# A two-block transformer kernel: inh, the gate weights and the ring 96 bytes further on in SBUF, everything behind them 128 bytes

## The chip, the core and the metric

The kernel runs on one core of one Trainium2 chip. The metric is the device time of one execution in microseconds; lower is better. The kernel before takes 1469.38 us, the median of three runs.

## What is computed

The reference takes one sequence of 256 tokens with 1024 features in float32 through two blocks and normalises at the end. The first block is an RWKV-7 recurrence beside a sparse attention with compressed, selected and window branches, and a gated feed-forward layer. The second has two layers, one with a gated linear attention beside a softmax attention with forget gates ("even"), one with an attention over a selected latent ("odd"), with two half-weighted feed-forward layers in each. Cut to what carries the time:

```python
h = h + y @ w_out[i]
h = h + swiglu(rms_norm(h, norm2_g[i]), ffn_w_gate[i], ffn_w_up[i], ffn_w_down[i])
...
x = x + 0.5 * swiglu_2(rmsnorm(x, g[0]), ffn_w_in[layer, 0], ffn_w_out[layer, 0])
h = rmsnorm(x, g[1])
x = x + even_mixer(h, ...)   # or odd_mixer
x = x + 0.5 * swiglu_2(rmsnorm(x, g[2]), ffn_w_in[layer, 1], ffn_w_out[layer, 1])
```

There are five feed-forward layers, each with a hidden width of 2816, and three input projections (w_in, even_in, odd_in) with an output projection each.

## The kernel before

All weights come as one stream of slots of 128 x 3072 floats (12,288 bytes in a partition) through a ring of four slots in SBUF, loaded by the SyncE queue; a slot is loaded again when its user frees it. The five engines run programs written out by hand, tied by semaphores.

A float32 product is made of three passes over split operands. ScalarE copies a block of weights, rounded to the type fp32r, out of the ring (the high half). VectorE subtracts that from the block, which leaves the low half. The activations are split in the same way: uT_h lies in the tensor uT, uT_l in yT. The passes are high weights by high activations, low by high, high by low. Where the halves lie depends on the stage:

- w_in: high in `in_h` (the tensor inh), low written back into the ring, `ring_r` (hi_block L1289, lo_block L1946). In its column items the weights are stationary and uT, 256 columns, is moving; in its token items it is the other way round. 22 column items of 24 matmuls each and two token items of 24.
- even_in and odd_in: high in `even_h` and `odd_h`, which lie in the scratch tensor wk, low in `ring_r`.
- output projections: high in `out_h` (in wk), low in `ring_r`; both moving, 512 columns, with uT stationary.
- feed-forward layers (five times 22 chunks): both halves in `w_gu` and `w_dn`, which lie in wk. A chunk is 48 matmuls with w_gu stationary and uT moving (256 columns), then 12 with the hidden values `h_r` (in ffb) stationary and w_dn moving (512 columns). ScalarE copies the high half (L1303, L1309), VectorE subtracts (L1953, L1959).

Almost all matmuls are issued by the helper at L440, so groups are told apart by their tiles: in "ps<-uT_h,w_gu" ps is the PSUM bank that is written, the others are the two operands.

inh, gate_r and the ring are used as scratch too: inh holds attention scores and probabilities outside w_in. The SBUF tensors are laid down one after the other with the helper `sb`; views made with `over` (in_h, ring_r, w_gu, h_r and so on) move with the tensor under them. The allocator rounds each start up to a multiple of 32 bytes.

Of the kernel before, what the change touches and what calls it, by code (L numbers as in the profile page):

```python
# [15 lines left out]
P = 128  # L16
# [76 lines left out]
def build(nc, x_in, wstream, gains, consts_in, masks_in, scratch, out):  # L93
    ctx = ExitStack()
    with ctx:
        at = {}

        def sb(name, shape, dt=F32):
            at[name] = nc.sbuf_base
            return ctx.enter_context(nc.sbuf_tensor(name, shape, dt))  # L100
# [19 lines left out]
        xn = sb("xn", [P, TT, D])  # L120
        uT = sb("uT", [P, KC, T])
        yT = sb("yT", [P, KC, T])
        inh = sb("inh", [P, KC * 3 * P])
        gb = inh[:, 0:2 * D].rearrange("p (a b) -> p a b", b=D)
        sb("gate_r", [P, 2 * KC * 24])
        ring = sb("ring", [P, RING, SLOT])
        ffb = sb("ffb", [P, 4, T])
        cst = sb("cst", [P, NCONST])
        msk = sb("msk", [P, MASKS], U8)
# [2549 lines left out]
```

## Time and profile before

| | |
|---|---|
| median of three runs | 1469.38 us (1469.09 to 1470.21) |
| the profiled execution | 1469.0 us |
| its span | 1467.2 us |
| TensorE matmul busy | 1427.4 us (97%) |
| weight loads busy | 1313.1 us (89%) |
| VectorE busy | 958.4 us (65%) |
| ScalarE busy | 698.3 us (48%) |
| read from HBM | 235.89 MB, 162 GB/s over the span |

In the profile PE is TensorE's matmuls, PEld its weight loads, DVE VectorE, ACT ScalarE, SP the queue that issues the transfers. L440 is line 440 of the kernel. Times in the timeline count from the span's start. Matmuls are pipelined: the printed duration of one is modelled, and the distance from one start to the next is what it costs in a dense stretch.

### The profile page before, as it was taken

To read this page: it belongs to the slowest core of one execution; us is meant where nothing else is said; L and a number is where in the kernel's file an instruction comes from. 1 tells how busy PE (TensorE), PEld (TensorE's weight loads), DVE (VectorE), ACT (ScalarE), POOL (GpSimd) and SP (SyncE) were. 2 spreads that over 40 slices of the span, in tenths; PEclk is the share of its full clock that TensorE was granted. 3 is DMA by queue.
4 is the path that set the end of the run, shared out by engine and by line. 5 is a ranking of instruction groups with operands and counts; after the bars stand their busy time and mean duration, and the time that the engine had idled before them with its cause. 6 is when DMAs were issued, how large, how long until landed. Compare 5 with 4: busy or idle time off the path is not lost. (4 is left out here: it accounts for less than half of the span.)

```text
span 1467.2 us, 26041 instructions
## 1 busy us (share of the span) xinstructions
PE 1427.4 (97%) x10266; PEld 1313.1 (89%) x10266; DVE 958.4 (65%) x1559; ACT 698.3 (48%) x1119; POOL 86.9 (6%) x140
## 2 busy tenths in 40 slices
PE   8998999999999999999999999999999999999998
PEld 7886998899998999989989999999999878899997
DVE  4766657766667766666467666676665667576665
ACT  6763444543345434457564434353433656544342
POOL 2040001000002000010000000010000114000000
PEclk9999999999999999999999999999999999999999
DMA  8343001654553545424336545445545423455440
GB/s 347 142 157 130 1 1 44 244 212 175 186 201 130 216 176 201 180 96 163 130 121 246 193 176 201 182 166 184 205 176 189 161 86 140 149 216 195 172 171 29
DMA packets 26575, 238.06 MB, mean 162 GB/s; under 512 B 2544, under 2 KB 6784, under 8 KB 7808
## 3 DMA queue, kind: packets, MB, share of 16 engines
q1 hardware_dynamic: 23824, 233.39, 43.1%
q10 hardware_dynamic: 2672, 3.58, 0.7%
q8 instruction: 53, 0.87, 0.2%
q14 instruction: 26, 0.21, 0.0%
HBM read 235.89 MB, written 1.07 MB: 162 GB/s over the span
## 5 line engine op out<-in xcount | busy, mean ns | idle before, releaser
L440 PE MATMUL ps<-uT_h,w_gu 128*128 128x256 f32 x3520 | 614.1, 279 | 0.4 <-DVE w_gu L1953 0.4
L440 PEld LDWEIGHTS ps<-uT_h,w_gu 128*128 128x128 f32 x3520 | 537.7, 188 | 11.0 <-issue 1.4
L440 PE MATMUL ps<-uT_l,w_gu 128*128 128x256 f32 x1760 | 478.8, 279 | 0.0
L440 PE MATMUL ps<-w_dn,h_r 128*128 128x512 f32 x1320 | 326.2, 396 | 0.3 <-DVE h_r L1995 0.3
L440 PEld LDWEIGHTS ps<-uT_l,w_gu 128*128 128x128 f32 x1760 | 325.4, 188 | 0.0
L440 PEld LDWEIGHTS ps<-w_dn,h_r 128*128 128x128 f32 x1320 | 239.4, 188 | 51.2 <-issue 1.7
L1303 ACT CAST w_gu<-ring 128x2048 fp32r<-128x2048 f32 x110 | 209.9, 1909 | 154.9 <-PE ps L440 154.8
L1953 DVE TENSOR_TENSOR w_gu<-ring,w_gu 128x2048 fp32r<-128x2048 f32 x110 | 252.1, 2292 | 34.5 <-ACT w_gu L1303 34.1
L1986 DVE TENSOR_TENSOR us<-ps,bc 128x256 f32<-128x256 f32 x110 | 46.5, 422 | 202.6 <-PE ps L440 202.5
L1316 ACT ACTIVATE wk<-wk 128x256 f32<-128x256 f32 x110 | 46.1, 419 | 261.4 <-DVE wk L1984 261.4
L1309 ACT CAST w_dn<-ring 128x1024 fp32r<-128x1024 f32 x110 | 115.6, 1051 | 82.9 <-PE ps L440 82.7
L1959 DVE TENSOR_TENSOR w_dn<-ring,w_dn 128x1024 fp32r<-128x1024 f32 x110 | 134.1, 1219 | 5.3 <-ACT w_dn L1309 5.1
L440 PE MATMUL ps<-uT_h,ring_r 128*128 128x256 f32 x408 | 114.3, 281 | 0.0
L440 PE MATMUL ps<-wk 128*128 128x128 f32 (+6 forms) x624 | 96.0, 305 | 9.8 <-ACT wk L1437 3.0
L440 PEld LDWEIGHTS ps<-wk 128*128 128x128 f32 (+3 forms) x624 | 73.1, 187 | 18.5 <-ACT wk L1437 5.1
L440 PEld LDWEIGHTS ps<-uT_h,ring_r 128*128 128x128 f32 x408 | 77.5, 190 | 0.3
L1984 DVE TENSOR_TENSOR wk<-ps,bc 128x256 f32<-128x256 f32 x110 | 46.7, 425 | 37.9 <-PE ps L440 22.7
L440 PE MATMUL ps<-ring_r,uT_h 128*128 128x512 f32 (+2 forms) x176 | 62.0, 352 | 0.0
L440 PE MATMUL ps<-uT_h,in_h 128*128 128x256 f32 x176 | 50.7, 290 | 2.5 <-PE ps L440 1.2
L1989 DVE TENSOR_TENSOR wk<-wk,us 128x256 f32<-128x256 f32 x110 | 46.7, 425 | 7.7 <-ACT wk L1316 4.2
L1789 POOL TENSOR_SCALAR small<-small 128x1 f32<-128x1 f32 (+3 forms) x19 | 9.2, 482 | 687.1 <-ACT xn L1247 483.6
L1995 DVE TENSOR_TENSOR h_r<-wk,h_r 128x256 fp32r<-128x256 f32 x110 | 46.8, 425 | 3.8
(385 smaller groups left out, 1789.0 us busy)
## 6 DMA issues: line engine op xcount, KB each, us to landing
ring<-wstream SPq DMA_DIRECT2D x144, 1536.0 KB, 6.2
cst<-consts_in SPq DMA_DIRECT2D x1, 2185.0 KB, 13.7
wk<-t_row ACTq DMA_DIRECT2D x1, 2048.0 KB, 7.8
wk<-masks_in SPq DMA_DIRECT2D x1, 1216.0 KB, 24.0
x<-x_in SPq DMA_DIRECT2D x2, 512.0 KB, 4.6
ring<-wstream SPq DMA_DIRECT2D x1, 1024.0 KB, 8.7
inh<-gains ACTq DMA_DIRECT2D x2, 512.0 KB, 9.5
out_dram<-x SPq DMA_DIRECT2D x3, 256.0 KB, 2.1
```

The source lines that it names most:

```text
L440: return pe.matmul(o, l, r, start=start, stop=stop, skip_group_check=True)
L1303: act.copy(w_gu[:, c % 2, 0, :], slot(i)[:, 0:2 * D]).then_inc(s["hi_a"], 1)
L1309: act.copy(w_dn[:, c % 2, 0, :], slot(i)[:, 2 * D:3 * D]).then_inc(s["hi_b"], 1)
L1316: act.activation(sg[:, c % 2, :], sg[:, c % 2, :], ACT.Silu).then_inc(s["silu_ready"], 1)
L1789: G(gp.tensor_scalar(o, i, scale, eps, ALU.mult, ALU.add))
L1953: v.tensor_tensor(w_gu[:, c % 2, 1, :], slot(i)[:, 0:2 * D], w_gu[:, c % 2, 0, :].bitcast(F32), ALU.subtract).then_inc(s["lo_a"], 1)
L1959: v.tensor_tensor(w_dn[:, c % 2, 1, :], slot(i)[:, 2 * D:3 * D], w_dn[:, c % 2, 0, :].bitcast(F32), ALU.subtract).then_inc(s["lo_b"], 1)
L1984: v.tensor_tensor(h, ps[4 + c % 2][:, 0:T], bc[:], ALU.mult).then_inc(s["gs_ready"], 1)
L1986: v.tensor_tensor(us[:], ps[6 + c % 2][:, 0:T], bc[:], ALU.mult).then_inc(s["us_ready"], 1)
L1989: v.tensor_tensor(h, h, us[:], ALU.mult).then_inc(s["h_mul"], 1)
L1995: v.tensor_tensor(hr[:, 1, :], h, hr[:, 0, :].bitcast(F32), ALU.subtract).then_inc(s["h_ready"], 1)
```

## The change

Two unused tensors are laid between others: one of 24 floats (96 bytes in a partition) ahead of inh, one of 8 floats (32 bytes) behind the ring. So inh, gate_r and the ring start 96 bytes later, and ffb, cst, msk, small, wk and everything after them 128 bytes later. x, xn, uT and yT stay where they are.

```diff
         uT = sb("uT", [P, KC, T])
         yT = sb("yT", [P, KC, T])
+        sb("space_w", [P, 24])
         inh = sb("inh", [P, KC * 3 * P])
         gb = inh[:, 0:2 * D].rearrange("p (a b) -> p a b", b=D)
         sb("gate_r", [P, 2 * KC * 24])
         ring = sb("ring", [P, RING, SLOT])
+        sb("space_f", [P, 8])
         ffb = sb("ffb", [P, 4, T])
         cst = sb("cst", [P, NCONST])
```

## Rows read from the trace of the kernel before

**Rows 1.** The page, busy time: engine, us, share, instructions.

```profile
PE 1427.4 (97%) x10266; PEld 1313.1 (89%) x10266; DVE 958.4 (65%) x1559; ACT 698.3 (48%) x1119; POOL 86.9 (6%) x140
```

**Rows 2.** Costliest groups: form and count, busy us, mean ns, idle before.

```profile
L440 PE MATMUL ps<-uT_h,w_gu 128*128 128x256 f32 x3520 | 614.1, 279 | 0.4 <-DVE w_gu L1953 0.4
...
L440 PE MATMUL ps<-uT_l,w_gu 128*128 128x256 f32 x1760 | 478.8, 279 | 0.0
L440 PE MATMUL ps<-w_dn,h_r 128*128 128x512 f32 x1320 | 326.2, 396 | 0.3 <-DVE h_r L1995 0.3
```

**Rows 3.** Timeline, a feed-forward chunk: start us, duration us, engine, line, operands, count.

```profile
598.75 0.28 PE L440 MATMUL ps<-uT_l,w_gu 128*128 128x256 f32 x1
...
601.55 0.27 PE L440 MATMUL ps<-uT_l,w_gu 128*128 128x256 f32 x1
601.66 0.39 PE L440 MATMUL ps<-w_dn,h_r 128*128 128x512 f32 x1
...
604.47 0.40 PE L440 MATMUL ps<-uT_h,w_gu 128*128 128x256 f32 x2
```

**Rows 4.** Timeline, a column item of w_in.

```profile
63.84 0.28 PE L440 MATMUL ps<-uT_l,in_h 128*128 128x256 f32 x1
...
65.28 0.28 PE L440 MATMUL ps<-uT_l,in_h 128*128 128x256 f32 x1
```

**Rows 5.** Timeline, a token item of w_in.

```profile
100.78 0.28 PE L440 MATMUL ps<-ring_r,uT_h 128*128 128x256 f32 x1
...
101.86 0.28 PE L440 MATMUL ps<-ring_r,uT_h 128*128 128x256 f32 x1
```

**Rows 6.** Timeline, column items of even_in.

```profile
649.75 0.28 PE L440 MATMUL ps<-uT_l,even_h 128*128 128x256 f32 x1
...
651.51 0.28 PE L440 MATMUL ps<-uT_l,even_h 128*128 128x256 f32 x1
```

**Rows 7.** Groups kept apart by form, whole span: loads from the ring and in_h.

```profile
L440 PE MATMUL ps<-uT_h,ring_r 128*128 128x256 f32 x408 | 114.3, 281 | 0.0
...
L440 PE MATMUL ps<-uT_h,in_h 128*128 128x256 f32 x176 | 50.7, 290 | 2.5 <-PE ps L440 1.2 <-DVE ring_r L1946 1.2
...
L440 PE MATMUL ps<-ring_r,uT_h 128*128 128x512 f32 x96 | 37.8, 394 | 0.0
```

**Rows 8.** The same view from 40 to 103 us.

```profile
L440 PE MATMUL ps<-uT_h,in_h 128*128 128x256 f32 x128 | 37.1, 290 | 1.2 <-PE ps L440 1.2
...
L440 PE MATMUL ps<-in_h,uT_h 128*128 128x256 f32 x16 | 4.7, 294 | 0.6 <-DVE ring_r L1946 0.6
```

**Rows 9.** Waits of TensorE, 40 to 95 us: us in total, times, longest.

```profile
PE ps L440 <- PE ps L440: 1.5, 5, 0.3
...
PEld ps L440 <- ACT xn L1374: 0.6, 3, 0.2
```

**Rows 10.** Timeline, the first matmuls of a w_in item after a gap.

```profile
75.33 0.28 PE L440 MATMUL ps<-uT_h,ring_r 128*128 128x256 f32 x1
...
76.28 0.28 PE L440 MATMUL ps<-uT_h,in_h 128*128 128x256 f32 x1
```

**Rows 11.** Timeline, the output projection of the even mixer.

```profile
746.38 0.40 PE L440 MATMUL ps<-out_h,uT_h 128*128 128x512 f32 x1
...
748.48 0.40 PE L440 MATMUL ps<-out_h,uT_h 128*128 128x512 f32 x1
```

**Rows 12.** VectorE's split of the weights, groups by form, whole span.

```profile
L1946 DVE TENSOR_TENSOR ring_r<-ring,in_h 128x1024 fp32r<-128x1024 f32 x24 | 29.7, 1244 | 15.0 <-ACT in_h L1289 14.1 <-DVE wk L2034 0.6
...
L1946 DVE TENSOR_TENSOR ring_r<-ring,even_h 128x1024 fp32r<-128x1024 f32 x24 | 28.6, 1222 | 8.9 <-ACT even_h L1289 8.6
```

**Rows 13.** Stretches: PE, PEld, DVE, ACT, POOL busy us (count), clock, DMA share, GB/s.

```profile
11.00:13.00 2.00, 2.00 (x20) 2.00 (x19) 0.00 (x0) 0.21 (x1) 0.00 (x0) 1.00 1.02 430
14.00:18.00 4.00, 4.00 (x34) 3.90 (x34) 4.00 (x16) 4.00 (x14) 0.00 (x0) 1.00 1.02 437
...
300.00:400.00 100.00, 100.00 (x716) 93.45 (x715) 64.42 (x84) 40.61 (x36) 0.00 (x0) 1.00 0.52 189
```

## Prediction

> **What bounds the kernel now.** I read the page first. TensorE is busy for 97% of the span and VectorE for 65% [rows 1]; the idle time of TensorE's largest groups is 0.4 us or less for each [rows 2]. So time is made or lost where the spacing of matmuls changes; a change in VectorE, ScalarE or DMA time counts only where it is large. The granted clock is 1.00 of full speed in all stretches that I asked for [rows 13], so the clock is no part of this. Busy time is of little help here, because an end of a matmul is modelled: I read the distance from start to start in the timeline.
>
> That distance is the point. With the weights in w_gu, 24 matmuls of 256 columns start within 601.55 - 598.75 = 2.80 us, 116.7 ns each [rows 3]. With the weights in in_h and ring_r, same shapes, same moving tile uT, 12 start within 65.28 - 63.84 = 1.44 us, 120.0 ns each [rows 4]; in the token items, where the same two tiles are the moving ones, 9 start within 101.86 - 100.78 = 1.08 us, again 120.0 ns [rows 5]. In the even mixer, where two of three matmuls load even_h and one loads ring_r, 15 start within 651.51 - 649.75 = 1.76 us, 117.3 ns [rows 6]. Nothing waits in any of these stretches.
>
> What differs is where the tiles begin. Worked out from the shapes (buffers are laid down one after the other, each start rounded up to 32 bytes), x, xn, uT, yT, inh, gate_r, ring, ffb and cst all begin at the same place modulo 128 bytes; call it 0. cst is 4662 x 4 = 18,648 bytes, which is 88 over a multiple of 128; rounded up to 32 that puts msk, small, wk and all that follows at +96. So w_gu, w_dn, even_h, odd_h and out_h (all in wk) sit 96 past uT, and in_h and ring_r sit level with it. The 120 ns go with "level", the 116.7 ns with "96 apart", and the mixture lies between.
>
> **The change part by part.** No instruction is added, removed, moved or made to wait, no DMA is added, and the two new tensors are never touched. Five things move.
>
> 1. inh and gate_r by 96 bytes: in_h goes from level to +96 against uT. That is the relation of w_gu now, to which the 116.7 ns belong. The saving is 3.3 ns a matmul. The w_in stage has 176 matmuls of each of three kinds for its columns [rows 7] and 16 of each of three for its tokens [rows 8]: 576, at most 1.9 us. Is TensorE the bound there? Between 40 and 95 us its matmuls wait 1.5 us for its own earlier ones, and of other engines its weight loads wait for ScalarE, 0.6 us in the larger case [rows 9], so nearly all arrives. Two discounts: after a gap the spacing needs some matmuls to settle at 120 (8 in 76.28 - 75.33 = 0.95 us, 118.8 ns) [rows 10], so I take 3.0 ns for the 384 + 48 matmuls after 40 us [rows 8]: 1.3 us. The other 144, before 40 us, run beside the loading of the constants and stop for VectorE's split of the weights, 1.2 us in all [rows 7]; I take half of 0.45 us, 0.2 us.
>
> 2. The ring by 96 bytes, as the low half of the weights (ring_r). It is in item 1 for w_in. In the even and odd mixers 408 - 176 = 232 matmuls load it between twice as many from wk [rows 7]; the mixed spacing of 117.3 should fall to 116.7. By the row that is 0.6 ns x 696 (three passes of 232) = 0.4 us; by a third of 3.3 ns it is 0.8 us. I take 0.6 us.
>
> 3. The ring as the moving operand of the output projections, 96 matmuls of 512 columns [rows 7]. Their stationary tile is uT, so here too level becomes 96 apart, and rows speak mildly against it: nine matmuls, a third of them from ring_r, take 748.48 - 746.38 = 2.10 us, 233.3 ns each [rows 11], while the down projection, moving w_dn at +96 over h_r at 0, takes 604.47 - 601.66 = 2.81 us for 12, 234.2 ns [rows 3]. If all 288 go to 234.2 that costs 0.9 x 288 = 0.26 us. I take 0.3 us lost; the bounds are 0 and 1.0 us (96 times the 10 ns by which the printed distances differ).
>
> 4. ffb, cst, msk, small, wk and the rest by 128 bytes. Modulo 128 nothing changes, and the two relations that make up the feed-forward time, w_gu against uT and w_dn against h_r, stay 96 apart. Both h_r and w_dn move by the same 128. I take nothing. No row shows a step of 128 bytes alone, so this is the widest unknown: bounded by the slowest spacing seen for this shape, (120.0 - 116.7) x 5280 = +17.4 us, and on the other side, if the effect could be as much the other way, -17.4 us. I take 0 because within one matmul the weights run through 512 bytes and the moving rows through 1024, so both pass every multiple of 128 in any case; only the part below 128 differs lastingly.
>
> 5. The ring and inh as operands of VectorE, ScalarE and DMA. VectorE's subtraction of 1024 elements takes 1244 ns on average with both inputs level (in_h) and 1222 with the second at +96 (even_h) [rows 12]: 22 ns on each of 24 is 0.5 us of VectorE, which is busy for 65% and seldom waited for here. The DMA engines move 430 GB/s while the ring fills from its level start and 437 while mostly the constants land in cst, whose loaded part begins 16 bytes past a multiple of 128 [rows 13]: no cost of an odd start to be seen. In the feed-forward stages the queue is busy for 0.52 of the time [rows 13], so even 10% more would be covered. Taken at 0, bounds -0.3 and +0.5 us, the latter a tenth of some 5 us in which the first matmuls wait for data.
>
> The sum is -1.3 - 0.2 - 0.6 + 0.3 = -1.8 us. The profiled execution took 1469.0 us with a span of 1467.2; it should become 1467.2 with a span of 1465.4. Taken off the median of 1469.4 it gives 1467.6 us, 0.12% less. What a measurement of this kernel can tell from no change is about 0.2%, 2.9 us; the forecast lies below that.
>
> **The rivals.**
> (a) The start has nothing to do with it: the 120 ns belong to the w_in stage, not to its tiles. For it: no row of w_in shows its high weights in another place. Against it: the spacing is the same in the column items, the token items and beside quite different neighbours, and the even mixer, with the same code and one third of the tiles, is at 117.3. Time: 1469.4. The same time results if item 1 is right but the gain is lost again behind w_in, where a later stage may wait for another engine than TensorE. The Trainium skill speaks for this rival: "SBUF — State Buffer", section Who interferes with whom, gives TensorE a read port for moving rows and an independent one for weights, and says that it never waits on anyone; by that no start address could matter and the sum would be 0. Rows 3 and 4 do not agree with the rule as far as it is read that way.
>
> (b) Slower: the period of the effect is 256 or 512 bytes, not 128. Then w_gu against uT changes after all (from 32 bytes below to 96 above, modulo 512: wk begins 18,656 + 2,304 + 1,024 = 21,984 bytes behind cst, 32 short of 43 x 512, and all from uT to cst is a multiple of 512), and the 5280 feed-forward matmuls may fall into the 120 ns pattern: +17.4 - 1.8 = +15.6 us, 1485.0. Even 0.9 ns on each (4.8 us) turns the sign beyond what can be measured. For it: no row holds w_gu at another multiple of 128. Against it: 24 feed-forward matmuls keep 116.7 ns on average [rows 3] while both streams step through all multiples of 512 from one k to the next, and the even mixer lies near them [rows 6].
>
> (c) Clearly faster: the same mechanism with the other sign, or the level start also slows the scratch uses of inh and ring in attention. The first, at 1 ns on each of the 5280, is 5.3 us; 1469.4 - 5.3 - 1.8 = 1462.3. For it: no row excludes the sign. Against it: the same as against (b).
>
> **How the numbers follow.** Forecast (a gain of 0.5 to 2.8 us): 0.57. Rival (a), nothing: 0.16. Rival (b), slower: 0.13. Rival (c): 0.14, of which 0.02 would still be within 0.2%. The forecast's own tail beyond 2.9 us is 0.03. So faster by over 0.2%: 0.12 + 0.03 = 0.15; slower by over 0.2%: 0.13; within: 0.72. The forecast's own range is 1466.4 to 1468.9. The range that should hold 8 in 10 takes in (a), the measuring scatter of 1.1 us in the three runs, and the near ends of (b) and (c): 1464.5 to 1470.8.
>
> **What the profile after would show.** Items 1 and 2: starts in w_in 116.7 ns apart, and in the even mixer too. Item 3: the ring_r matmuls of 512 columns some 3 ns further apart. Item 4: 24 feed-forward matmuls in 2.80 us and 12 of the down projection in 2.81, as now. Item 5: VectorE's subtraction and the DMA rates as in rows 12 and 13. The forecast is wrong if w_in stays at 120.0 (rival a), or if the feed-forward distance moves by even 1 ns (b or c), which alone is worth 5.3 us.

## The result, and the profile after

The changed kernel takes 1478.54 us (median of five, 1477.71 to 1479.02) against 1469.55 us: the ratio is 1.0059, 95% interval 1.0048 to 1.0071. It is slower by 9 us where I had forecast a gain of 1.8 us and 1467.6, with a range up to 1470.8. What happened is rival (b) in kind, at 0.6 of the price that I had put on it.

The page after (engine, busy us, share of the span, instructions):

```profile
span 1476.5 us, 26041 instructions
...
PE 1436.8 (97%) x10266; PEld 1323.0 (90%) x10266; DVE 958.9 (65%) x1559; ACT 698.7 (47%) x1119; POOL 86.9 (6%) x140
```

Against [rows 1] VectorE, ScalarE and GpSimd are where they were, within 0.5 us; TensorE is busy 9.4 us longer, and the span is 9.3 us longer (1467.2 before). The number of instructions is the same. The costliest groups after (form and count, busy us, mean ns, idle before), which answer to [rows 2]:

```profile
L442 PE MATMUL ps<-uT_h,w_gu 128*128 128x256 f32 x3520 | 623.5, 281 | 0.3 <-DVE w_gu L1955 0.3
...
L442 PE MATMUL ps<-uT_l,w_gu 128*128 128x256 f32 x1760 | 482.0, 281 | 0.0
...
L442 PE MATMUL ps<-w_dn,h_r 128*128 128x512 f32 x1320 | 325.6, 395 | 0.2 <-DVE h_r L1997 0.2
```

The idle time before these groups is as small as before. The loss is in the spacing, the time from one matmul's start to the next one's. The timeline after, a feed-forward chunk, as in [rows 3]:

```profile
599.00 0.28 PE L442 MATMUL ps<-uT_l,w_gu 128*128 128x256 f32 x1
...
601.85 0.28 PE L442 MATMUL ps<-uT_l,w_gu 128*128 128x256 f32 x1
```

Eight groups of three, 24 matmuls, in 2.85 us: 118.8 ns instead of the 116.7 of [rows 3]. And a column item of w_in, as in [rows 4]:

```profile
63.50 0.28 PE L442 MATMUL ps<-uT_l,in_h 128*128 128x256 f32 x1
...
64.91 0.28 PE L442 MATMUL ps<-uT_l,in_h 128*128 128x256 f32 x1
```

12 matmuls in 1.41 us, 117.5 ns in this item instead of 120.0.

Summed from each start to the next over the whole trace, and as the mean spacing where matmuls follow densely, the two kernels stand like this (worked out from the starts):

| matmuls | count | before | after | difference |
|---|---|---|---|---|
| w_gu by uT | 5280 | 620.1 us, 116.7 ns | 629.8 us, 118.6 ns | +9.7 us |
| w_dn by h_r | 1320 | 311.0 us, 233.3 ns | 310.3 us, 232.7 ns | -0.7 us |
| in_h by uT, stationary | 352 | 49.0 us, 119.8 ns | 48.8 us, 118.6 ns | -0.2 us |
| ring_r by uT, stationary | 408 | 48.5 us, 118.8 ns | 48.3 us, 118.3 ns | -0.2 us |
| even_h, odd_h by uT, stationary | 464 | 65.4 us, 117.4 ns | 65.7 us, 118.3 ns | +0.3 us |
| ring_r, 512 columns | 96 | 24.3 us, 231.3 ns | 24.6 us, 234.4 ns | +0.3 us |
| out_h, 512 columns | 192 | 46.3 us, 234.3 ns | 46.0 us, 232.7 ns | -0.3 us |

The rest moves by 0.1 us or so a group. The first line has 9.7 us; all other groups together give 0.4 us back, which leaves the 9.3 us of the span.

### The profile page after: what moved, and what is told of

The parts are those of the page before. It is cut to its first block and busy times, and to the rows that moved or that the text cites. A ratio compares the mean times of both kernels' runs of the same rounds, so it can differ in the third digit from the quotient of the medians.

```text
span 1476.5 us, 26041 instructions
## 1 busy us (share of the span) xinstructions
PE 1436.8 (97%) x10266; PEld 1323.0 (90%) x10266; DVE 958.9 (65%) x1559; ACT 698.7 (47%) x1119; POOL 86.9 (6%) x140
## 5 line engine op out<-in xcount | busy, mean ns | idle before, releaser
L442 PE MATMUL ps<-uT_h,w_gu 128*128 128x256 f32 x3520 | 623.5, 281 | 0.3 <-DVE w_gu L1955 0.3
```

The costliest lines, as they stand in the source:

```text
L442: return pe.matmul(o, l, r, start=start, stop=stop, skip_group_check=True)
```

## The experiments

In what follows "w_gu is 32 below uT" means: the start of the weights less the start of the moving rows, modulo 256 bytes, is 256 - 32 = 224. For the down projection the same words give the start of the moving w_dn less that of the stationary h_r. All experiments are the kernel before with other padding, except the two that add matmuls behind its last layer.

### The two halves of the change, and everything moved together

The first half alone; ffb, wk and the rest are brought to the same place modulo 512 (kcT and gtok are taken from their places further down, gtok in the last run too):

```diff
+        sb("space_w", [P, 24])
         inh = sb("inh", [P, KC * 3 * P])
...
         ring = sb("ring", [P, RING, SLOT])
+        kcT = sb("kcT", [P, 2, 16])
+        gtok = sb("gtok", [P, TT, 24])
+        sb("space_f", [P, 24])
```

> The first pad alone: inh, gate_r and the ring 96 bytes further on; kcT, gtok and more padding are laid behind the ring, so that ffb, cst, wk and all behind move by 512 bytes and keep their place modulo 512. Theory 1 (the loss is all in wk's move by 128 bytes; the period of the effect is a multiple of 128 that divides 512): the feed-forward distance stays at 116.7 ns, w_in falls from 119.8 to 118.6 ns as in the changed kernel, and the time is 0 to 1 us below the kernel before. Theory 2 (the loss is in the ring, which ScalarE and VectorE read while TensorE runs): about 1478, the feed-forward distance at 118.6.

Measured: 1469.26 us, ratio 0.9997 (0.9988 to 1.0007). Its timeline, a feed-forward chunk:

```profile
597.61 0.28 PE L442 MATMUL ps<-uT_l,w_gu 128*128 128x256 f32 x1
...
600.76 0.28 PE L442 MATMUL ps<-uT_l,w_gu 128*128 128x256 f32 x1
```

27 matmuls in 3.15 us, 116.7 ns, as in [rows 3]. in_h went from 119.8 to 118.2 ns and the whole w_in stage gained 0.6 us by its starts. So the part of my forecast that held is this small.

The second half alone:

```diff
         ring = sb("ring", [P, RING, SLOT])
+        sb("space_f", [P, 32])
```

> The second half alone: inh and the ring stay, ffb, cst, wk and all behind move by 128 bytes. Theory 1: the feed-forward distance goes to 118.6 ns and the time to about 1479, nearly 10 us above the kernel before. Theory 2: 1469.5, no change.

Measured: 1478.52 us, ratio 1.0061 (1.0044 to 1.0077), the whole loss. The same stretch:

```profile
599.55 0.28 PE L441 MATMUL ps<-uT_l,w_gu 128*128 128x256 f32 x1
...
602.39 0.28 PE L441 MATMUL ps<-uT_l,w_gu 128*128 128x256 f32 x1
```

24 in 2.84 us, 118.3 ns here and 118.5 over the trace. Theory 2 (the loss comes from the ring's place) falls with both runs: the ring moved in the first and nothing was lost, it stayed in the second and all was.

Everything moved by 128 bytes:

```diff
+        sb("space_x", [P, 32])
         x = sb("x", [P, TT, D])
```

> 128 bytes ahead of x, so that every tensor moves by 128 and no distance between two tensors changes. Theory 1a (what counts is the weights' start relative to the moving rows' start): no change, 1469.5, feed-forward distance 116.7 ns. Theory 1b (what counts is the absolute place of the weights modulo 256 or 512): as the changed kernel, near 1478, 118.6 ns.

Measured: 1469.66 us, ratio 1.0001 (0.9991 to 1.0011), and

```profile
598.05 0.28 PE L441 MATMUL ps<-uT_l,w_gu 128*128 128x256 f32 x1
...
601.90 0.28 PE L441 MATMUL ps<-uT_l,w_gu 128*128 128x256 f32 x1
```

33 in 3.85 us, 116.7 ns. Here wk lies where the changed kernel has it, and costs nothing: what counts is not the place but the distance between the two tiles that TensorE reads at once. Theory 1b (the absolute place) falls.

### The sweep, and the period

The cases added behind the last layer (x and y count steps of 32 bytes, 8 floats; fq is w_gu flat, fr are uT_h and uT_l flat, fd is w_dn flat):

```diff
+            def case(x, y):
...
+                banks += 1
+                for n in range(2):
+                    mm(ps[6][:, :], h_r[:, 0, 0, 0:P], w_dn[:, 0, 0, n * 512:(n + 1) * 512], n == 0, n == 1)
+                for m in range(2):
+                    for k in range(7):
+                        for n, (a, b) in enumerate(PASSES):
+                            lo = 8 * x + a * 2 * D + (m * KC + k) * P
+                            mm(ps[4 + banks % 2][:, 0:T], fq[:, lo:lo + P], fr[b][:, 8 * y + k * T:8 * y + (k + 1) * T],
+                               k == 0 and n == 0, k == 6 and n == 2)
+            for c in range(16):
+                case(c, 0)
+            for c in range(16):
+                case(0, c)
+            for c in range(16):
+                for n in range(16):
+                    lo = 8 * c + n % 2 * 512 + n // 4 % 2 * 1024
+                    mm(ps[6][:, :], h_r[:, 0, n % 2, n // 8 * P:n // 8 * P + P], fd[:, lo:lo + 512], n == 0, n == 15)
...
```

> The kernel before with some 1700 more matmuls behind its last feed-forward layer, which change no result. 16 cases of 42 matmuls of the feed-forward form, with w_gu read 0, 32, ... 480 bytes further on; 16 with uT further on by as much; 16 of 16 matmuls of the down projection with w_dn further on. Theory 1a: case 4 of the first sweep (128 bytes) shows 118.6 ns, case 0 116.7, case 1 (level with uT) about 120, and the second sweep mirrors the first. Theory 1b: the second sweep, where the weights stay, is flat. Theory 2: both are flat at 116.7. The time is about 230 us longer for the added work.

The spacing of the 16 cases with w_gu further on, in ns: 116.7, 119.8, 118.3, 117.7, 117.3, 118.7, 119.7, 113.3, and then the same eight again within 0.2. Two of them in the timeline, level with uT and 64 below it:

```profile
1466.78 0.28 PE L440 MATMUL ps<-uT_l,w_gu 128*128 128x256 f32 x1
...
1470.37 0.28 PE L440 MATMUL ps<-uT_l,w_gu 128*128 128x256 f32 x1
```

```profile
1499.45 0.28 PE L440 MATMUL ps<-uT_l,w_gu 128*128 128x256 f32 x1
...
1503.19 0.28 PE L440 MATMUL ps<-uT_l,w_gu 128*128 128x256 f32 x1
```

30 in 3.59 us, 119.7 ns, and 33 in 3.74 us, 113.3 ns. With uT further on: 116.7, 117.8, 120.1, 118.6, 118.9, 117.8, 118.3, 119.8, repeated. For most distances the two sweeps agree (level 119.8 and 119.8; 32 above 118.3 and 118.3; 128 apart 118.7 and 118.6); at two they don't: 96 above shows 117.3 in one and 118.9 in the other, 64 below 113.3 and 117.8. The down projection, w_dn against h_r in eight steps from 32 below: 232.9, 228.5, 232.9, 233.3, 233.9, 231.9, 234.1, 233.3; level is the best here, by 3.4 ns. So theory 1a (the distance counts) held for the period and the direction but not for one value per distance; case 4 gave 117.3 where I had written 118.6.

The period in the whole kernel, with only what lies behind ffb moved by 256 bytes:

```diff
         ffb = sb("ffb", [P, 4, T])
+        sb("space_k", [P, 64])
```

> Only what lies behind ffb (cst, msk, small, wk, misc) moves, by 256 bytes. The sweep repeats itself after 8 steps of 32 bytes. Theory 1 (period of 256 bytes in the distance of weights and moving rows): feed-forward distance 116.7 ns, time 1469.5, as before. Rival (period of 512, of which the sweep showed two like halves by chance): another distance than 116.7 and a time over 5 us away.

Measured: 1469.69 us, ratio 1.0000 (0.9990 to 1.0009), spacing 116.7 ns. The period of 256 bytes stands.

### One distance, two spacings

The cases of the sweep again, of 21 matmuls each, over all 64 pairs of places, in two orders and behind two or three down matmuls:

```diff
+            for lw in range(8):
+                for mv in range(8):
+                    case(lw, mv, 2)
+            for mv in range(8):
+                for lw in range(8):
+                    case(lw, mv, 3)
```

> The kernel before with 128 cases of 21 matmuls of the feed-forward form behind its last layer, which change no result: w_gu 0 to 224 bytes further on by uT 0 to 224 further on, in two orders and behind two or three matmuls of 512 columns. Theory 1a (only the difference counts): the spacing is the same along every diagonal. Theory 1c (the difference chooses among a few patterns, and how a run begins decides which one holds): some diagonals hold two values, and the second order may show others than the first; among them the one with 118.6 ns in the changed kernel and 117.3 in the sweep.

Measured: sorted by distance, 16 cases each, the spacings fall into these (worked out from the starts, from the third matmul of a case on):

| w_gu against uT | spacings in ns, and how often |
|---|---|
| 32 below (before) | 116.4 to 117.1 (12), 117.8 (4) |
| level | 119.2 to 120.0 (16) |
| 32 above | 118.2 to 118.4 (16) |
| 64 above | 113.3 to 114.3 (9), 117.7 or 117.8 (7) |
| 96 above (changed) | 117.2 to 117.4 (10), 118.5 to 118.9 (6) |
| 128 apart | 118.4 to 119.1 (11), 119.8 to 120.0 (5) |
| 96 below | 119.3 to 120.0 (16) |
| 64 below | 117.8 or 117.9 (15), 113.3 (1) |

The same two addresses (w_gu one step on, uT six) in the first order and in the second:

```profile
1503.79 0.28 PE L440 MATMUL ps<-uT_l,w_gu 128*128 128x256 f32 x1
...
1505.83 0.28 PE L440 MATMUL ps<-uT_l,w_gu 128*128 128x256 f32 x1
```

```profile
1806.73 0.28 PE L440 MATMUL ps<-uT_l,w_gu 128*128 128x256 f32 x1
...
1808.85 0.28 PE L440 MATMUL ps<-uT_l,w_gu 128*128 128x256 f32 x1
```

18 matmuls in 2.04 us and in 2.12 us, 113.3 and 117.8 ns. What ran ahead of them differs, and so does the PSUM bank that they write, since the cases take two banks in turn. At 96 above the bank is the same in both orders, and there too one pair of addresses shows two values: w_gu six steps on and uT two is at 117.2 ns in the first order and 118.5 in the second (worked out from the starts). So a distance admits one pattern or two, and the addresses do not settle which. That what runs ahead picks is what is left; each order ran once, and chance is only made unlikely: in the sweep cases 8 to 15 repeat cases 0 to 7 within 0.2 ns, the rare 113.3 ns at 64 below included.

### Trying the distances in the real layers

wk alone, by 224 bytes (w_gu 64 below uT):

```diff
         ffb = sb("ffb", [P, 4, T])
+        sb("space_k", [P, 56])
```

> Only what lies behind ffb moves, by 224 bytes, case 7 of the first sweep (113.3 ns). Theory 1: 5280 x (116.7 - 113.3) = 18 us less, near 1451.6; the down projection stays at 233.3 ns. Rival (what the sweep showed holds only behind the kernel, where VectorE, ScalarE and the ring are idle): less than half of that gain.

Measured: 1475.29 us, ratio 1.0040 (1.0025 to 1.0054), and 117.8 ns in all five layers. The 18 us did not come. The map explains it: at this distance 15 of 16 cases are at 117.8, and the sweep had shown me the rare one.

in_h, ring_r and w_gu all 64 below uT, and w_dn level with h_r:

```diff
+        sb("space_w", [P, 48])
         inh = sb("inh", [P, KC * 3 * P])
...
         ffb = sb("ffb", [P, 4, T])
+        sb("space_k", [P, 8])
```

> inh, the ring, ffb and cst 192 bytes further on, wk and what follows 224, so that in_h, ring_r, h_r and wk all lie 64 below uT modulo 256 and w_dn lies level with h_r. Theory 1: the 18 us of the run with wk alone; 1320 x (233.3 - 228.5) = 6.3 us in the down projection; (119.8 - 113.3) x 576 = 3.7 us in w_in and about 2.5 in the other two projections: near 1439. Rival as in that run: between 1455 and 1465.

Measured: 1469.60 us, ratio 1.0001 (0.9991 to 1.0011). By the starts w_gu lost 6.0 us (117.8 ns), the down projection gained 4.7 (229.7 ns) and the input projections about 1.5: three terms that nearly cancel in the time and can only be told apart by the spacing.

The changed kernel with w_dn level with h_r:

```diff
+        sb("space_w", [P, 24])
         inh = sb("inh", [P, KC * 3 * P])
...
         ffb = sb("ffb", [P, 4, T])
+        sb("space_k", [P, 8])
```

> The changed kernel, but ffb follows the ring by 96 bytes too (32 bytes of the padding lie behind ffb), so that w_dn begins level with h_r and w_gu still 96 above uT. Theory 3 (the distance of w_gu and uT admits a few patterns, 117.3 and 118.7 ns at this one, and the way a run begins, behind other down matmuls, picks one): the down projection falls from 232.7 to about 228.6 ns, 1320 x 4.1 = 5.4 us, and w_gu is at 117.3 or at 118.7: 1466 or 1473. Rival (the distance fixes the spacing alone): 118.6 as in the changed kernel, 1473.

Measured: 1474.35 us, ratio 1.0031 (1.0021 to 1.0041): the down projection at 228.4 ns, as expected, and w_gu at 118.7 in all layers. This run does not tell theory 3 from its rival, since both allowed for the value.

wk alone by 128 bytes, ffb not:

```diff
         ffb = sb("ffb", [P, 4, T])
+        sb("space_k", [P, 32])
```

> Only what lies behind ffb moves, by 128 bytes: w_gu against uT goes from 32 below to 96 above as in the changed kernel, while w_dn against h_r changes from 32 below to 96 above too, which the changed kernel leaves alone. Theory 1 (the distance of w_gu and uT is the cause): feed-forward distance 117.3 or 118.7 ns, time 1473 or 1479. Rival (it is the joint move of ffb and wk): 116.7 and about 1469.5. The sweep of the down projection gives 233.9 ns for it at this distance, under 1 us more.

Measured: 1476.13 us, ratio 1.0046 (1.0029 to 1.0062). Neither 1473 nor 1479, for the pattern changes from layer to layer: the third layer and the second,

```profile
806.06 0.28 PE L441 MATMUL ps<-uT_l,w_gu 128*128 128x256 f32 x1
...
810.28 0.28 PE L441 MATMUL ps<-uT_l,w_gu 128*128 128x256 f32 x1
```

```profile
609.17 0.28 PE L441 MATMUL ps<-uT_l,w_gu 128*128 128x256 f32 x1
...
612.73 0.28 PE L441 MATMUL ps<-uT_l,w_gu 128*128 128x256 f32 x1
```

36 in 4.22 us, 117.2 ns, against 30 in 3.56 us, 118.7 ns. Layers one, three, four and five run at 117.3, the second at 118.7. So the distance of w_gu and uT alone makes the feed-forward layers slower, by 4.7 us here; the joint move of ffb is not needed for a loss. It matters in a second way: part2_only differs from this run in the place of ffb alone, which puts w_dn 32 below h_r as in the changed kernel, and there all five layers take the slower of the two patterns, which makes the loss 9.3 us by w_gu.

wk alone by 96 bytes (w_gu 64 above uT, w_dn 64 above h_r):

```diff
         ffb = sb("ffb", [P, 4, T])
+        sb("space_k", [P, 24])
```

> Only what lies behind ffb moves, by 96 bytes: w_gu 64 above uT, the distance at which the map showed both 113.4 and 117.8 ns. Theory 3: one of the two holds in all of the five layers, so 1469.5 - 17.4 = 1452 or 1469.5 + 5.8 = 1475. Rival (distance alone): something between the two.

Measured: 1450.77 us (1449.97 to 1453.80), ratio 0.9866 (0.9850 to 0.9883), 19 us faster than the kernel before. The profiled execution is the longest of the four, 1453.80 us. In it, the first layer and the second:

```profile
411.97 0.28 PE L441 MATMUL ps<-uT_l,w_gu 128*128 128x256 f32 x1
...
416.05 0.28 PE L441 MATMUL ps<-uT_l,w_gu 128*128 128x256 f32 x1
```

```profile
602.94 0.28 PE L441 MATMUL ps<-uT_l,w_gu 128*128 128x256 f32 x1
...
605.76 0.28 PE L441 MATMUL ps<-uT_l,w_gu 128*128 128x256 f32 x1
```

36 in 4.08 us, 113.3 ns, against 24 in 2.82 us, 117.5 ns. Four layers are fast and the second slow. My expectation that one pattern would hold in all five was wrong, and that the time lies near my 1452 is partly luck: of the 15.2 us that the profiled execution gained, w_gu has 10.3 and the down projection, from which I had expected nothing, 4.9 (worked out from the starts). Its 12 matmuls in a chunk of the first layer:

```profile
416.16 2.91 PE L441 MATMUL ps<-w_dn,h_r 128*128 128x512 f32 x12
418.91 0.40 PE L441 MATMUL ps<-uT_h,w_gu 128*128 128x256 f32 x2
```

12 in 2.75 us, 229.2 ns, where the sweep had 233.3 for w_dn 64 above h_r. So the sweep's value for a distance need not hold in the layers for this form either.

The same distance of w_gu, in_h and ring_r at it too, but w_dn level with h_r:

```diff
+        sb("space_w", [P, 16])
         inh = sb("inh", [P, KC * 3 * P])
...
         ffb = sb("ffb", [P, 4, T])
+        sb("space_k", [P, 8])
```

> inh, the ring, ffb and cst 64 bytes further on, what lies behind 96: w_gu, in_h and ring_r 64 above uT, w_dn level with h_r. Theory 3: the down projection at 228.6 ns, 6 us less; w_gu at 113.4 or 117.8, not necessarily as in the run with wk alone, since the matmuls ahead differ: 1446 or 1469.

Measured: 1463.15 us, ratio 0.9952 (0.9935 to 0.9968): the slower pattern in all layers but for the first chunks (117.8 ns), the down projection at 227.0, in_h at 115.7.

in_h and ring_r brought to 32 below uT, where w_gu is, and w_dn level with h_r:

```diff
+        sb("space_w", [P, 56])
         inh = sb("inh", [P, KC * 3 * P])
...
         ffb = sb("ffb", [P, 4, T])
+        sb("space_k", [P, 8])
```

> inh, the ring, ffb and cst 224 bytes further on, what lies behind 256: in_h, ring_r and w_gu all 32 below uT modulo 256 (w_gu as in the kernel before), w_dn level with h_r. Theory 3: w_gu at 116.7 or 117.8 ns, the two values of this distance on the map; with 116.7 the gain is 6 us in the down projection and 2 to 3 us in the input projections, near 1461; with 117.8 it is 1467.

Measured: 1462.69 us, ratio 0.9948 (0.9932 to 0.9965), w_gu 116.7 ns and the down projection 228.8: the first of the two cases, near 1461.

Last, the fast pattern with the input projections drawn to it:

```diff
+        sb("space_w", [P, 16])
         inh = sb("inh", [P, KC * 3 * P])
...
         ring = sb("ring", [P, RING, SLOT])
+        gtok = sb("gtok", [P, TT, 24])
         ffb = sb("ffb", [P, 4, T])
+        sb("space_k", [P, 24])
```

> The run with wk by 96, with the input projections drawn level: inh and the ring 64 bytes further on, ffb and wk where they are in that run modulo 256 (256 and 352 bytes further on, gtok laid between for room). Theory 3: the five layers as in that run, four of them at 113.3 ns and one at 117.8 or all five at 113.3; w_in and the others at 115.7 instead of 119.8 and 118.4 ns, 576 x 4 + 696 x 2.7 = 4 us less: 1446.5, or 1442 with the fifth layer. Rival (any change ahead of a layer can tip it): one or more further layers at 117.8, 4.7 us each, 1451 or more.

Measured: 1447.74 us (1446.51 to 1448.79), ratio 0.9853 (0.9836 to 0.9869), 1.5% faster than the kernel before and 2.1% faster than the changed one. The second layer now:

```profile
597.85 0.28 PE L442 MATMUL ps<-uT_l,w_gu 128*128 128x256 f32 x1
...
601.25 0.28 PE L442 MATMUL ps<-uT_l,w_gu 128*128 128x256 f32 x1
```

30 in 3.40 us, 113.3 ns. Every feed-forward distance is that of the run with wk by 96, and the second layer has tipped to the fast side: from its first start to its last it takes 183.9 us, against 187.8 there. That the input projections tipped it is not shown. The other three executions of wk_by_96 are 2.8 to 3.8 us shorter than the profiled one, which is about what one layer is worth; they left no trace, so the same kernel may take either pattern from one execution to the next.

## Why the prediction was wrong

**What bounds the kernel** was right: all 9.3 us lie in the spacing of dense matmuls, and neither another engine nor the queue shows in them. As forecast, VectorE's split of in_h takes 1248 ns (1244 in [rows 12]), and the DMA engines move 442 and 428 GB/s in the stretches of [rows 13], 430 and 437 before.

**Item 4 is the step that failed.** It took the distance modulo 128, for which no row spoke: [rows 3 to 6] hold two distances, level and 32 below, and any period from 64 bytes up would have fitted them. The two arguments that I brought are void. That both streams pass every multiple of 128 within a matmul says nothing on how they lie to each other as they do; and that the spacing stays put over the steps of k tests multiples of 512 only. It is 256 bytes (wk_by_256, the sweep), and the change took w_gu from 32 below to 96 above: 118.6 ns in place of 116.7, on 5280 matmuls, 9.7 us where the sum had nothing. Moving wk alone by 128 bytes cost w_gu 4.7 us of these; the rest came with the slower of the two patterns at that distance, of which no row knew. The bound of +17.4 us held; the chance of 0.13 for it did not do justice to an unknown that stands on 5280 matmuls without a row.

**Items 1 and 2** were right in sign and too large. I took the spacing of w_in to become 116.7, the value for 32 below. At 96 above it becomes 118.6, or 118.2 where the first half was tried alone, so w_in and its ring matmuls gained 0.4 us and not 1.5; and the other two projections, where even_h and odd_h moved with wk, lost 0.4 us instead of gaining 0.6 (and another 0.4 in their token items, which the sum left out). The same mistake of the period, at about a fifth of the size (2.1 us off in all).

**Item 3**: the ring's matmuls of 512 columns cost 0.3 us, as forecast, and out_h gave 0.3 us back. **Item 5**: nothing, as forecast.

**The rivals.** (a) falls: part1_only changed in_h's spacing by moving it. (b) is what happened, with 118.6 ns in place of the 120.0 by which I priced it, since each distance has values of its own. (c) did not happen here, but wk_by_96 shows that the sign is open: wk 32 bytes short of where the change put it, with inh, the ring and ffb left in place, wins 19 us.

**Left open:** what exactly picks between the two patterns, and whether it picks alike in each execution. Shown is that the distance sets which there are, that the same addresses take either, and that in each trace a layer may waver in its first four chunks and then keeps its mean spacing within 0.1 ns for the other 18. That w_dn level with h_r goes with the slow one, and w_dn further above it with the fast one, holds in changed_level, plus_64, fast_start and most layers of wk_by_128 and wk_by_96, but the second layers of these two break it.

## What to carry to other kernels

Where TensorE is the bound and loads new weights for every matmul, do not take padding for neutral: in this kernel paddings alone gave times from 1447.7 to 1478.5 us. Note for each hot pair the start of the weights less the start of the moving rows modulo 256, measure the eight values in steps of 32 bytes in the kernel itself, and read the spacing from start to start, since several such terms can cancel in the time. Of an effect seen at two distances claim no period; a step that moves the operand of most matmuls needs a row, or the weight in the chances that its count gives it. And take a probe's single good value for what may hold, not for what will: the fast pattern has to be looked for in each layer of the profile, and the single times beside the median.

## What the runs showed of the hardware

The spacing of 256-column matmuls with fresh 128-column weights runs from 113.3 to 120.0 ns at a granted clock of 1.00. It goes by the distance of the two tiles modulo 256 bytes and, at some distances, by something that the addresses do not settle, most likely what ran ahead; moving every tensor by 128 bytes changes nothing (ratio 1.0001). The other engines are not needed for it: the added cases ran with VectorE, ScalarE and GpSimd idle and fall on the same values as the layers. With 512 columns the range is 227.0 to 235 ns. Level was the best place in the sweep (228.5) and gave 227.0 to 229.7 in the layers, a place where the 256-column form is near its worst (119.8); but 64 above gave 229.2 to 229.5 in the layers of wk_by_96 too. The Trainium skill ("SBUF — State Buffer", section Who interferes with whom) has TensorE's two read ports independent and TensorE waiting for no one; if that is to cover the two against each other, these runs do not agree with it.

Two patterns at one distance, 4.5 ns apart and each stable over the last 18 chunks of 60 matmuls in a layer, I had not expected at all. A layer that tips changes the kernel's time by about 4 us (187.8 against 183.9 us for the second layer).
